# GLA state block on TensorE: a chunk's four attention products ahead of its four state products, one opening product per PSUM bank

## The chip, the cores and the metric

The kernel runs on one NeuronCore of a Trainium2 chip. The metric is the device time of one execution in microseconds (us); lower is better. Times of several runs are given as a median.

## What is computed

The reference is one layer of a decoder trunk with four parallel token mixers over 1024 tokens and 1024 features. The mixer that matters here is gated linear attention (GLA), 4 heads, key width 64, value width 128, run chunk by chunk. Cut to what matters (`qt`, `kt`, `vt` are a chunk's queries, keys and values, `cum` the running sum of the log gates, `decay` its causal differences):

```
o_inter = einsum('bhtk,bhkv->bhtv', qt * exp(cum), state)
att     = einsum('bhtk,bhsk,bhtsk->bhts', qt, kt, decay)
o       = o_inter + einsum('bhts,bhsv->bhtv', att, vt)
state   = exp(last) * state + einsum('bhsk,bhsv->bhkv', kt * exp(last - cum), vt)
```

So each chunk's output of each head is a sum of two matrix products: attention weights times values, contracted over the chunk's tokens, and the decayed queries times the state, contracted over the 64 key features. Then each head is normalised, gated and stored.

## The kernel before

The program runs in blocks, one after another, with a barrier of all engines between two blocks: the front (projections, convolution), stick-breaking attention, GLA, windowed attention, the merge and the MLP. Through the middle blocks TensorE also works off the gate projection, `Dense` (names `dn_...`), in pieces: `dense.pieces(pe, 1)` issues 6 or 9 instructions of `split_product` (lines 661 to 663, 128x512 each), while `dense.serve` on ScalarE copies finished halves out and splits the next weights (lines 156 and 135), `dense.lower` on GpSimd makes their low part (line 139) and `dense.move` on the SP queue stores and loads. Where a piece stands between other work is written out by hand in each block.

`stage_gla` has four blocks: preparation, the attention levels (line 1836, into `gl_ps_att`), the **state block** (lines 1886 to 1955) and the norm block (lines 1957 on). A chunk is 128 tokens (`CH`), so there are `N_CH` = 8. Head h has the numbers c = h // 2 and r = h % 2. A head's 64 key features lie in partitions 0 to 63 for r = 0 and 64 to 127 for r = 1.

In the state block the order on TensorE is, for n = 0 to 7:

1. `update(n)` (n < 7, line 1909): four products of keys and values into `gl_ps_u`. Each uses 64 columns of the array: head r writes partitions 64r to 64r + 63. The first weight load waits for `state_ready`.
2. for n < 6 one piece of the gate projection;
3. waits for `o_copied` (the output bank of chunk n - 2 copied out by ScalarE) and for `state_ready` (both halves of the state before chunk n);
4. for each of four heads an **attention product** (line 1926, `gl_ps_o<-gl_att,gl_v_tok`, all 128 rows of the array) and, for n >= 1, a **state product** (line 1929, `gl_ps_o<-gl_q_decayed,gl_state`, 64 rows of the array) that accumulates on it. Heads with r = 0 write one PSUM bank, heads with r = 1 another; the two heads of a bank (c = 0, 1) write its columns 0 to 127 and 128 to 255. The last product increments `o_done`.

VectorE makes the next state from `update(n)` once the outputs of chunk n - 1 are done (lines 1942, 1945; two instructions a chunk). ScalarE copies each chunk's output to `gl_oT` (line 1953). An fp32 product shows in the profile as two instructions (passes), so a chunk's 8 products are 16 rows. In the profile `64*128` in front of a shape means 64 rows and 128 columns of the array, `128*64` means 128 rows and 64 columns.

The norm block then runs, per head, Square and three other instructions on ScalarE (lines 1981 to 1984), a sum on TensorE over the squares (line 1999) after two pieces of the gate projection, and Ln and Exp of that sum on ScalarE (lines 1986, 1987).

Of the kernel before, what the change touches and what calls it, by code (L numbers as in the profile page):

```python
# [13 lines left out]
P = 128  # L14
# [35 lines left out]
def sems(nc, ctx, *names):  # L50

    Kernel.in_use += [nc.alloc_semaphore(n) for n in names]
    return Kernel.in_use[-len(names):]
# [9 lines left out]
def feature_tiles(ap):  # L63

    return ap.rearrange("(t p) c -> p t c", p=P)
# [1179 lines left out]
E = 64  # L1245
# [378 lines left out]
GLA_HEADS = 4  # L1624
GLA_TAU = 16.0
CH = P
# [4 lines left out]
def stage_gla(nc, k, w_gate, dense):  # L1631
# [7 lines left out]
    with ExitStack() as outer:  # L1639
        def hold(name, shape, dt=F32):  # L1640
            return outer.enter_context(nc.sbuf_tensor(name, shape, dt))
# [4 lines left out]
        q_in = hold("gl_q_decayed", [P, 2, S])  # L1646
        k_tok = hold("gl_k_tok", [P, N_CH, 2 * P])
        v_tok = hold("gl_v_tok", [P, N_CH, GLA_HEADS * P])
        last_decay = hold("gl_last", [P, 2, N_CH])
        with ExitStack() as ctx:  # L1650
# [14 lines left out]
            @block.sync  # L1665
            def _(sp):
                sp.wait_ge(k.stick_stored, 32)
                dense.finish(sp, dense.first_gate - R_CONV)
                sp.dma_start(low[:, :], k.proj[R_LOW * P:R_LOW * P + RANK, :]).then_inc(low_in, 16)
                sp.dma_start(wg[:, :], w_gate[0]).then_inc(low_in, 16)  # L1670
                sp.dma_start(vT[:, :, :], feature_tiles(k.proj[R_CV * P:(R_CV + 4) * P, :])).then_inc(v_in, 16)
                sp.dma_start(q[:, :, :], feature_tiles(k.proj[R_CQ * P:(R_CQ + 2) * P, :])).then_inc(qk_in, 16)
                sp.dma_start(kk[:, :, :], feature_tiles(k.proj[R_CK * P:(R_CK + 2) * P, :])).then_inc(qk_in, 16)
                dense.move(sp, FROM + PREPARE)
# [91 lines left out]
        att = hold("gl_att", [P, N_CH // 2, 2, HALF])  # L1766
# [115 lines left out]
        with ExitStack() as late:  # L1882
# [3 lines left out]
            with ExitStack() as ctx:  # L1886
                state = ctx.enter_context(nc.sbuf_tensor("gl_state", [P, 2, 2, P], F32))
                ps_o = ctx.enter_context(nc.psum_tensor("gl_ps_o", [P, 2, 2, HALF], F32))
                ps_u = ctx.enter_context(nc.psum_tensor("gl_ps_u", [P, 2, HALF], F32))
                update_done, state_ready, o_done, o_copied = sems(nc, ctx, "gl_update_done", "gl_state_ready", "gl_o_done", "gl_o_copied")  # L1890
                block = ctx.enter_context(nc.Block())

                @block.sync
                def _(sp):
                    sp.dma_start(rT[:, :, :], feature_tiles(k.proj[R_CR * P:(R_CR + 4) * P, :])).then_inc(r_in, 16)
                    dense.move(sp, FROM + PREPARE + LEVEL + STATE)

                @block.gpsimd
                def _(pool):
                    dense.lower(pool, FROM + PREPARE + LEVEL + STATE)  # L1900

                @block.tensor
                def _(pe):
                    def update(n):
                        if n >= 2:
                            pe.wait_ge(state_ready, 2 * (n - 1))
                        for h in range(GLA_HEADS):
                            c, r = h // 2, h % 2
                            last = nc.tensor.matmul(ps_u[E * r:E * r + E, n % 2, c * P:(c + 1) * P],
                                                    k_tok[:, n, c * P + E * r:c * P + E * r + E], v_tok[:, n, h * P:(h + 1) * P],  # L1910
                                                    start=True, stop=True)
                        last.then_inc(update_done, 1)

                    for n in range(N_CH):
                        if n < N_CH - 1:
                            update(n)
                        if n < 3 * STATE:
                            dense.pieces(pe, 1)
                        if n >= 2:
                            pe.wait_ge(o_copied, n - 1)  # L1920
                        if n >= 1:
                            pe.wait_ge(state_ready, 2 * n)
                        for h in range(GLA_HEADS):
                            c, r = h // 2, h % 2
                            dst = ps_o[:, n % 2, r, c * P:(c + 1) * P]
                            last = nc.tensor.matmul(dst, v_tok[:, n, h * P:(h + 1) * P],
                                                    att[:, n // 2, r, (2 * (n % 2) + c) * P:(2 * (n % 2) + c + 1) * P], start=True, stop=(n == 0))
                            if n >= 1:
                                last = nc.tensor.matmul(dst, state[E * r:E * r + E, n % 2, c, :], q_in[E * r:E * r + E, c, n * CH:(n + 1) * CH],
                                                        start=False, stop=True)  # L1930
                        last.then_inc(o_done, 1)

                @block.vector
                def _(dve):
                    for n in range(N_CH - 1):
                        dve.wait_ge(update_done, n + 1)
                        if n >= 1:
                            dve.wait_ge(o_done, n)
                        for c in range(2):
                            new = state[:, (n + 1) % 2, c, :]  # L1940
                            if n == 0:
                                ins = nc.vector.tensor_copy(new, ps_u[:, n % 2, c * P:(c + 1) * P])
                            else:
                                dve.wait_ge(state_ready, 2 * n)
                                ins = nc.vector.scalar_tensor_tensor(out=new, in0=state[:, n % 2, c, :], scalar=last_decay[:, c, n:n + 1],
                                                                     in1=ps_u[:, n % 2, c * P:(c + 1) * P], op0=ALU.mult, op1=ALU.add)
                            ins.then_inc(state_ready, 1)

                @block.scalar
                def _(act):  # L1950
                    for n in range(N_CH):
                        act.wait_ge(o_done, n + 1)
                        nc.scalar.activation(oT[:, :, n * CH:(n + 1) * CH].rearrange("p (c r) t -> p r c t", r=2),
                                             ps_o[:, n % 2, :, 0:2 * P].rearrange("p r (c t) -> p r c t", t=P), ACT.Copy).then_inc(o_copied, 1)
                        dense.serve(act, FROM + PREPARE + LEVEL + min((n + 1) // 3, STATE))
# [379 lines left out]
```

## Time and profile before

| | |
|---|---|
| device time, median of 3 runs | 2219.93 us (2217.63 to 2221.23) |
| device time of the profiled execution | 2223.6 us |
| its span, first to last instruction | 2221.9 us |
| mean granted TensorE clock | 0.978 |
| TensorE (PE) busy | 2108.0 us, 95% of the span |
| VectorE (DVE) busy | 943.6 us, 42% |
| ScalarE (ACT) busy | 651.3 us, 29% |
| GpSimd (POOL) busy | 542.2 us, 24% |
| state block on TensorE | from 915.50 to about 955.1 us |

PEld is the loading of weights, which overlaps the products. The granted clock is a share of full speed: 1.00 is 2.4 GHz and 0.50 is 1.2 GHz. A busy time over a stretch shows occupancy only: two instructions that run beside each other, or one that waits in the pipe for another, count as busy all the same. Distances between the starts of two rows tell more, and the tables below are read in that way.

### The profile page before, as it was taken

The page shows a single profiled execution, that of the slowest core. Times are in us where ns is not written, and L with a number is a line of the kernel's source. Part 1 is how long each engine was busy: PE and PEld are TensorE (multiplying, and loading weights), DVE is VectorE, ACT ScalarE, POOL GpSimd, SP SyncE. Part 2 cuts the span into 40 slices and gives each one's busy share as a digit, 9 for nine tenths or more (in the row PEclk, how much of TensorE's full clock was granted, in tenths as well). Part 3 has the DMA queues.
Part 4 walks back from the last instruction along what each step waited for, and adds up shares of the span by engine and source line. Part 5 has one row for each costly group of instructions (what it writes and reads, how often), then busy time and mean ns, then how long its engine had stood idle before and what let it go on. Part 6 is the DMA issues. An engine that isn't in the chain of part 4 may idle for free. (4 is left out here: it accounts for less than half of the span.)

```text
span 2221.9 us, 23815 instructions
## 1 busy us (share of the span) xinstructions
PE 2108.0 (95%) x9584; PEld 1664.3 (75%) x9584; DVE 943.6 (42%) x1109; ACT 651.3 (29%) x913; POOL 542.2 (24%) x260
## 2 busy tenths in 40 slices
PE   6999999999999989988998799699999999999999
PEld 5878888787655668765787678478888888888887
DVE  6455753012333366333543368453343333334324
ACT  5311111233445222154653233232221221122111
POOL 0112222211211133014201011301343343333332
PEclk9999999999999989999999899899999999999999
DMA  8345553333111411235114476600111111111112
GB/s 276 100 139 167 151 152 95 91 106 122 38 42 39 153 57 39 77 106 193 37 59 142 145 239 218 255 20 20 48 48 48 48 48 57 48 39 52 53 48 95
DMA packets 200550, 216.99 MB, mean 98 GB/s; under 512 B 8778, under 2 KB 156362, under 8 KB 200442
## 3 DMA queue, kind: packets, MB, share of 16 engines
q1 hardware_dynamic: 200272, 215.40, 30.3%
q8 instruction: 77, 1.26, 0.2%
q14 instruction: 31, 0.25, 0.0%
q10 hardware_dynamic: 170, 0.07, 0.0%
HBM read 162.85 MB, written 52.59 MB: 97 GB/s over the span
## 5 line engine op out<-in xcount | busy, mean ns | idle before, releaser
L661 PE MATMUL dn_ps<-h_hi,dn_hi 128*128 128x512 f32 (+1 forms) x1120 | 470.5, 420 | 18.8 <-PEq L60 8.2
L663 PE MATMUL dn_ps<-h_hi,dn_lo 128*128 128x512 f32 (+1 forms) x1120 | 443.3, 396 | 0.0
L662 PE MATMUL dn_ps<-h_lo,dn_hi 128*128 128x512 f32 (+1 forms) x1120 | 442.9, 395 | 0.0
L139 POOL TENSOR_TENSOR dn_lo<-dn_raw,dn_hi 128x1024 fp32r<-128x1024 f32 (+1 forms) x69 | 166.0, 2406 | 691.2 <-ACT dn_hi L135 571.9
L661 PEld LDWEIGHTS dn_ps<-h_hi,dn_hi 128*128 128x128 f32 (+1 forms) x1120 | 213.0, 190 | 92.5 <-issue 41.6
L662 PEld LDWEIGHTS dn_ps<-h_lo,dn_hi 128*128 128x128 f32 (+1 forms) x1120 | 213.3, 190 | 49.5 <-issue 7.2
L663 PEld LDWEIGHTS dn_ps<-h_hi,dn_lo 128*128 128x128 f32 (+1 forms) x1120 | 212.5, 190 | 49.2
L1200 DVE TENSOR_TENSOR tl_x<-tl_x,tl_bank 128x512 f32<-128x512 f32 x256 | 173.2, 686 | 133.1 <-PE tl_bank L663 133.1
L156 ACT ACTIVATE dn_out<-dn_ps 128x512 f32<-128x512 f32 (+1 forms) x138 | 81.9, 593 | 476.3 <-PE dn_ps L663 469.9
L1036 POOL TENSOR_TENSOR tl_w_lo<-tl_raw,tl_w_hi 128x1024 fp32r<-128x1024 f32 x64 | 153.4, 2397 | 231.1 <-ACT tl_w_hi L957 231.1
L661 PE MATMUL tl_bank<-tl_h_hi,tl_w_hi 128*128 128x512 f32 x512 | 199.5, 390 | 0.0
L662 PE MATMUL tl_bank<-tl_h_lo,tl_w_hi 128*128 128x512 f32 x512 | 199.2, 389 | 0.0
L663 PE MATMUL tl_bank<-tl_h_hi,tl_w_lo 128*128 128x512 f32 x512 | 199.2, 389 | 0.0
L661 PE MATMUL tl_bank<-tl_w_hi,tl_u_hi 128*128 128x512 f32 x512 | 199.2, 389 | 0.0
L662 PE MATMUL tl_bank<-tl_w_lo,tl_u_hi 128*128 128x512 f32 x512 | 199.2, 389 | 0.0
L663 PE MATMUL tl_bank<-tl_w_hi,tl_u_lo 128*128 128x512 f32 x512 | 199.2, 389 | 0.0
L1042 POOL TENSOR_TENSOR tl_u_lo<-tl_square,tl_u_hi 128x1024 fp32r<-128x1024 f32 x32 | 104.3, 3259 | 277.5 <-DVE tl_square L1190 277.5
L1190 DVE TENSOR_TENSOR tl_square<-tl_relu 128x1024 f32<-128x1024 f32 x32 | 39.6, 1239 | 306.5 <-ACT tl_relu L988 306.5
L957 ACT ACTIVATE tl_w_hi<-tl_raw 128x1024 fp32r<-128x1024 f32 x64 | 67.8, 1061 | 286.2 <-PE tl_bank L663 226.6
L663 PEld LDWEIGHTS tl_bank<-tl_h_hi,tl_w_lo 128*128 128x128 f32 x512 | 96.1, 188 | 20.0
L661 PEld LDWEIGHTS tl_bank<-tl_h_hi,tl_w_hi 128*128 128x128 f32 x512 | 96.1, 188 | 20.0
L661 PEld LDWEIGHTS tl_bank<-tl_w_hi,tl_u_hi 128*128 128x128 f32 x512 | 96.1, 188 | 19.9
(281 smaller groups left out, 2969.3 us busy)
## 6 DMA issues: line engine op xcount, KB each, us to landing
dn_raw<-w_in_dram SPq DMA_DIRECT2D x70, 512.0 KB, 4.3
ada<-w_ada_dram SPq DMA_DIRECT2D x24, 1024.0 KB, 7.3
proj<-dn_out SPq DMA_DIRECT2D x72, 256.0 KB, 2.2
logits<-dn_out SPq DMA_DIRECT2D x64, 256.0 KB, 2.1
mg_gate<-logits SPq DMA_DIRECT2D x32, 512.0 KB, 5.1
tl_raw<-w_up_dram SPq DMA_DIRECT2D x32, 512.0 KB, 3.9
tl_raw<-w_down_dram SPq DMA_DIRECT2D x32, 512.0 KB, 3.5
wa_qk<-proj SPq DMA_DIRECT2D x6, 1024.0 KB, 16.5
```

Source lines behind the costliest of these rows:

```text
L139: self.nc.gpsimd.tensor_tensor(self.lo_at(j), self.raw_at(j), self.hi_at(j).bitcast(F32), ALU.subtract).then_inc(self.lo_ready, 1)
L156: self.nc.scalar.activation(self.out[0:width, h, :], self.ps[0:width, h, :], ACT.Copy).then_inc(self.copied, 1)
L661: nc.tensor.matmul(out, w_hi[:, t, :], x_hi[:, t, :], start=begin, stop=False)
L662: nc.tensor.matmul(out, w_hi[:, t, :], x_lo[:, t, :], start=False, stop=False)
L663: mm = nc.tensor.matmul(out, w_lo[:, t, :], x_hi[:, t, :], start=False, stop=end)
L957: nc.scalar.activation(dst, raw[:, ring(j)], ACT.Copy).then_inc(hi_ready, 1)
L1036: nc.gpsimd.tensor_tensor(lo, raw[:, ring(j)], hi.bitcast(F32), ALU.subtract).then_inc(lo_ready, 1)
L1042: nc.gpsimd.tensor_tensor(u_lo[:, b % 2, f, :], square[:, n % 2], u_hi[:, b % 2, f, :].bitcast(F32), ALU.subtract).then_inc(u_lo_ready, 1)
L1190: nc.vector.tensor_tensor(square[:, n % 2], relu[:, n % 2], relu[:, n % 2], ALU.mult).then_inc(square_ready, 1)
L1200: nc.vector.tensor_tensor(x1[:, tt, cols], x1[:, tt, cols], bank[:, 4 + n % 4, :], ALU.add).then_inc(summed, 1)
```

## The change

In step 4 the four attention products of a chunk now come first, then the wait for `state_ready`, then the four state products. The state products' order is h = 0, 1, 2, 3 as before, so r alternates 0, 1, 0, 1. Since the first product of a bank clears what is accumulated in the whole bank, only c = 0 opens (`start=(c == 0)`), and c = 1 writes its own columns without opening. The number of instructions and their operands stay; all other engines' code stays.

```
@@ -1918,16 +1918,17 @@
                             dense.pieces(pe, 1)
                         if n >= 2:
                             pe.wait_ge(o_copied, n - 1)
+                        for h in range(GLA_HEADS):
+                            c, r = h // 2, h % 2
+                            last = nc.tensor.matmul(ps_o[:, n % 2, r, c * P:(c + 1) * P], v_tok[:, n, h * P:(h + 1) * P],
+                                                    att[:, n // 2, r, (2 * (n % 2) + c) * P:(2 * (n % 2) + c + 1) * P],
+                                                    start=(c == 0), stop=(n == 0), skip_group_check=True)
                         if n >= 1:
                             pe.wait_ge(state_ready, 2 * n)
-                        for h in range(GLA_HEADS):
-                            c, r = h // 2, h % 2
-                            dst = ps_o[:, n % 2, r, c * P:(c + 1) * P]
-                            last = nc.tensor.matmul(dst, v_tok[:, n, h * P:(h + 1) * P],
-                                                    att[:, n // 2, r, (2 * (n % 2) + c) * P:(2 * (n % 2) + c + 1) * P], start=True, stop=(n == 0))
-                            if n >= 1:
-                                last = nc.tensor.matmul(dst, state[E * r:E * r + E, n % 2, c, :], q_in[E * r:E * r + E, c, n * CH:(n + 1) * CH],
-                                                        start=False, stop=True)
+                            for h in range(GLA_HEADS):
+                                c, r = h // 2, h % 2
+                                last = nc.tensor.matmul(ps_o[:, n % 2, r, c * P:(c + 1) * P], state[E * r:E * r + E, n % 2, c, :],
+                                                        q_in[E * r:E * r + E, c, n * CH:(n + 1) * CH], start=False, stop=True, skip_group_check=True)
                         last.then_inc(o_done, 1)
```

TensorE's order before, from the end of the state block's chunk 5 to the block's end (`x4` is four products of one kind in a row):

```order
L1909 MATMUL gl_ps_u<-gl_v_tok,gl_k_tok 64x128 x4
L1926 MATMUL gl_ps_o<-gl_att,gl_v_tok 128x128
L1929 MATMUL gl_ps_o<-gl_q_decayed,gl_state 128x128
L1926 MATMUL gl_ps_o<-gl_att,gl_v_tok 128x128
L1929 MATMUL gl_ps_o<-gl_q_decayed,gl_state 128x128
L1926 MATMUL gl_ps_o<-gl_att,gl_v_tok 128x128
L1929 MATMUL gl_ps_o<-gl_q_decayed,gl_state 128x128
L1926 MATMUL gl_ps_o<-gl_att,gl_v_tok 128x128
L1929 MATMUL gl_ps_o<-gl_q_decayed,gl_state 128x128
L1926 MATMUL gl_ps_o<-gl_att,gl_v_tok 128x128
L1929 MATMUL gl_ps_o<-gl_q_decayed,gl_state 128x128
L1926 MATMUL gl_ps_o<-gl_att,gl_v_tok 128x128
```

In each chunk from 1 to 7 the two kinds alternate product by product.

TensorE's order of the change at the same place, chunks 5, 6 and 7 and the barrier (line 1923 is the attention product, line 1930 the state product):

```order
L1923 MATMUL gl_ps_o<-gl_att,gl_v_tok 128x128 x4
L1930 MATMUL gl_ps_o<-gl_q_decayed,gl_state 128x128 x4
L1909 MATMUL gl_ps_u<-gl_v_tok,gl_k_tok 64x128 x4
L1923 MATMUL gl_ps_o<-gl_att,gl_v_tok 128x128 x4
L1930 MATMUL gl_ps_o<-gl_q_decayed,gl_state 128x128 x4
L1923 MATMUL gl_ps_o<-gl_att,gl_v_tok 128x128 x4
L1930 MATMUL gl_ps_o<-gl_q_decayed,gl_state 128x128 x4
L1886 UNCONDITIONAL_BRANCH
```

Eight changes of kind within a chunk have become two. Of the pieces of the gate projection and of `update` none has moved, and the other four engines' orders are the same.

## Rows read from the trace of the kernel before

**Rows 1.** The page: busy time, share and instructions of each engine.

```profile
PE 2108.0 (95%) x9584; PEld 1664.3 (75%) x9584; DVE 943.6 (42%) x1109; ACT 651.3 (29%) x913; POOL 542.2 (24%) x260
```

**Rows 2.** Waits in the state block (915 to 955.2 us): who, on whom, us, times, longest.

```profile
DVE gl_state L1945 <- PE gl_ps_u L1909: 28.8, 6, 5.4
ACT gl_oT L1953 <- PE gl_ps_o L1929: 27.0, 6, 5.4
```

**Rows 3.** Timeline of TensorE, chunk 0: start, us, engine, line, names, shape.

```profile
915.50 0.66 PE L1909 MATMUL gl_ps_u<-gl_v_tok,gl_k_tok 128*64 128x128 f32 x8 [1.65 <-PEq L1767]
...
918.27 1.05 PE L1926 MATMUL gl_ps_o<-gl_att,gl_v_tok 128*128 128x128 f32 x8
919.25 0.66 PE L1909 MATMUL gl_ps_u<-gl_v_tok,gl_k_tok 128*64 128x128 f32 x8
919.84 0.50 PE L661 MATMUL dn_ps<-h_hi,dn_hi 128*128 128x512 f32 x1
```

**Rows 4.** The same, chunk 1, first and last products, and what follows.

```profile
922.02 0.38 PE L1926 MATMUL gl_ps_o<-gl_att,gl_v_tok 128*128 128x128 f32 x2
922.34 0.49 PE L1929 MATMUL gl_ps_o<-gl_q_decayed,gl_state 64*128 64x128 f32 x2
...
925.25 0.66 PE L1909 MATMUL gl_ps_u<-gl_v_tok,gl_k_tok 128*64 128x128 f32 x8
```

**Rows 5.** The same, start of chunk 6, start of chunk 7, end of the block.

```profile
948.43 0.49 PE L1926 MATMUL gl_ps_o<-gl_att,gl_v_tok 128*128 128x128 f32 x2
...
951.76 0.49 PE L1926 MATMUL gl_ps_o<-gl_att,gl_v_tok 128*128 128x128 f32 x2
...
954.68 0.49 PE L1929 MATMUL gl_ps_o<-gl_q_decayed,gl_state 64*128 64x128 f32 x2
956.25 0.76 PE L661 MATMUL dn_ps<-h_hi,dn_hi 128*128 128x512 f32 x1 [1.09 <-PEq L1886]
```

**Rows 6.** Timeline of TensorE, windowed attention: products that alternate row halves.

```profile
1067.05 0.71 PE L1448 MATMUL wa_ps_s<-wa_qk 64*128 64x128 f32 x8 [2.53 <-PEq L1288]
1067.70 0.50 PE L661 MATMUL dn_ps<-h_hi,dn_hi 128*128 128x512 f32 x1
...
1105.79 1.30 PE L1448 MATMUL wa_ps_s<-wa_qk 64*128 64x128 f32 x8
1107.02 0.55 PE L1459 MATMUL wa_ps_t<-ident,wa_prob 128*128 128x128 f32 x3
```

**Rows 7.** Timeline of VectorE, state block: the state before chunk 7.

```profile
948.55 0.60 DVE L1945 SCALAR_TENSOR_TENSOR gl_state<-gl_state,gl_last,gl_ps_u 128x128 f32<-128x128 f32 x2 [4.70 <-PE gl_ps_u L1909]
```

**Rows 8.** Timeline of ScalarE, state block, after chunk 5.

```profile
947.95 0.60 ACT L1953 ACTIVATE gl_oT<-gl_ps_o 128x512 f32<-128x512 f32 x1 [4.71 <-PE gl_ps_o L1929]
948.44 0.59 ACT L156 ACTIVATE dn_out<-dn_ps 128x512 f32<-128x512 f32 x1
948.92 1.06 ACT L135 ACTIVATE dn_hi<-dn_raw 128x1024 fp32r<-128x1024 f32 x1
```

**Rows 9.** Stretches: us, busy PE, PEld, DVE, ACT, POOL (x instructions), granted clock, DMA share, GB/s.

```profile
951.80:955.20 3.40, 3.37 (x17) 2.33 (x16) 0.00 (x0) 0.60 (x1) 0.00 (x0) 1.00 0.00 0
955.20:956.20 1.00, 0.00 (x0) 0.00 (x0) 0.00 (x0) 0.71 (x2) 0.11 (x1) 0.67 0.00 0
956.20:959.00 2.80, 2.75 (x7) 2.20 (x8) 0.00 (x0) 2.77 (x3) 2.27 (x1) 0.50 0.00 0
...
973.80:975.40 1.60, 0.23 (x2) 0.03 (x1) 1.60 (x2) 1.60 (x3) 0.00 (x0) 1.00 1.12 332
...
991.70:994.60 2.90, 0.21 (x1) 0.00 (x0) 0.30 (x1) 1.54 (x2) 0.00 (x0) 1.00 0.61 242
```

**Rows 10.** Timeline of TensorE, norm block, pieces for the first head.

```profile
956.82 0.63 PE L662 MATMUL dn_ps<-h_lo,dn_hi 128*128 128x512 f32 x1
...
962.36 0.41 PE L663 MATMUL dn_ps<-h_hi,dn_lo 128*128 128x512 f32 x1
```

**Rows 11.** Timeline of ScalarE, norm block, Ln of the first head's sum.

```profile
965.22 1.12 ACT L1986 ACTIVATE gl_att<-gn_ps,eps 128x1024 f32<-128x1024 f32 x1 [4.96 <-PE gn_ps L1999]
```

## The prediction

> **What bounds the kernel now.** I began with the busy shares [rows 1]: TensorE is busy for 95% of the span and no other engine for half of it, so time taken off TensorE's stream comes off the whole, unless another wait takes its place. Next I asked who waits in the state block [rows 2]. VectorE and ScalarE wait for TensorE, 28.8 and 27.0 us in total; TensorE waits for neither of them there. The block is therefore as long as its row of products, and the timeline of TensorE is the view that matters. In it one looks at the distances between starts, since all these rows read as busy.
>
> **What the alternation costs.** In chunk 0 there is no state yet, and the four attention products run one behind another: from 918.27 to the start of the next kind at 919.25, 0.98 us [rows 3]. This takes in the change to the other kind of array shape that follows. In chunk 1 the eight alternating products run from 922.02 to 925.25, 3.23 us [rows 4]. A product costs 3.23 / 8 = 0.40 us there, against 0.98 / 4 = 0.245 us in chunk 0, although half of them use only half the rows. So what is paid for is the change of shape between full height and half height, eight times a chunk (the step to `update` is the eighth). The chunks 2 to 5 repeat this; chunk 6 runs from 948.43 to 951.76 and chunk 7 about as long, 3.33 us [rows 5], since they have no gate piece ahead and are entered through one more change of shape.
>
> **The change, part by part.**
>
> *Attention products together.* They become what chunk 0 has: 0.98 us, with the change of shape behind them [rows 3].
>
> *State products together, row halves alternating.* No place in the state block shows this. The nearest rows are in windowed attention, where four products of 64 rows and 128 columns alternate between the halves just as these will (h % 2, each half to banks of its own): 1067.05 to 1067.70, 0.65 us, with the change of shape behind them in it [rows 6]. Bounds: from below, `update`, four products that share the array by columns, 919.25 to 919.84, 0.59 us [rows 3]. From above, four products that share nothing: 0.98 us as in chunk 0, plus 0.10 us for entering from another shape (3.33 less 3.23), 1.08 us. Another row of the same line is dearer still, 1105.79 to 1107.02, 1.23 us [rows 6], but its operands are read with a step between elements, and `state` and `q_in` are read without one. I take 0.65: same shape, same alternation, same kind of access.
>
> *Sum.* A chunk's products fall from 3.23 to 0.98 + 0.65 = 1.63 us, by 1.60 us. In chunks 6 and 7 both sides carry the extra 0.10. Seven chunks: 7 x 1.60 = **11.2 us**. By the bounds it is 7 x (3.23 - 0.98 - 0.59) = 11.6 at best, 7 x (3.23 - 0.98 - 1.08) = 8.2 if the halves take turns, and 7 x (3.23 - 0.98 - 1.23) = 7.1 by the dearest row.
>
> The Trainium skill, page "TensorE: Matmul & The Clock Gate", section "Measured speedup vs the span model", gives a dimmer view of packing: four row tiles measured 3.07 times one, not 4. An estimate by that share (0.77) would make the paired products some 0.1 us dearer a chunk and the saving about 0.7 us smaller; the row at 1067.05 does not show such a loss.
>
> *The waits.* The wait for `o_copied` stays in front, the wait for `state_ready` moves back by 0.98 us, so neither can come to bind later than before by its place alone; but the block is shorter, so I follow both to the tightest chunk. The state before chunk 7 is made at 948.55, 0.12 us behind `update`, and takes 0.60 us [rows 7]. In the new order chunk 6's 1.7 us and chunk 7's attention products lie between, so it is ready some 2 us early. The output bank that chunk 7 wants is copied at 947.95 to 948.55 [rows 8], and chunk 7 starts about 1.7 us behind `update`. ScalarE then has 1.5 us of gate work queued, to 949.98 [rows 8]; chunk 6 would end at 948.43 + 1.73 = 950.2, and its copy is waited for by nobody before the end. Cover is thus there for all of VectorE's and ScalarE's work. If it were gone, the price is the 0.60 us of one copy. The increment of `o_done` is on the last product as before. Fewer changes of shape touch no queue, and nothing is moved past a DMA.
>
> *The clock behind the block.* After the last product, at 954.68, TensorE has nothing until 956.25 [rows 5], where the barrier ends. In that gap the granted clock goes from 1.00 to 0.50 (2.4 to 1.2 GHz) and stays low over the next pieces [rows 9]. Two gaps that are longer, 973.8 to 975.4 and 991.7 to 994.6, leave it at 1.00 [rows 9]. What differs is what the engine did before: there pieces of the gate projection without pause, here 6.7 us of alternation. In the new order the last two chunks are packed half as wide in time, so I expect the clock to stay. Price: between 956.25 and 962.36 there are 14 pieces' instructions in 6.11 us [rows 5, 10]; at full speed nine of them take 2.18 us (919.84 to 922.02, [rows 3, 4]), so 14 take 2.18 + 5 x 0.23 = 3.34. That is **2.8 us**, and it lies on the path, since ScalarE waited 4.96 us for the sum behind these pieces [rows 11].
>
> So 11.2 + 2.8 = 14.0 us. The profiled execution took 2223.6 us, which would become 2209.6. It is 3.7 us above the median of the runs, 2219.93, and 2.4 above the slowest; I carry the saving over to the median: 2219.93 - 14.0 = **2205.9 us**. The blocks that follow start from a barrier and are moved as a whole, so I take nothing off for them.
>
> **The rivals.**
>
> *The clock falls all the same* (or falls elsewhere instead). For it: the gap before the norm block stays 1.6 us long. Then only 11.2 us go: 2208.7 us. Chance 0.27.
>
> *The row halves take turns* while accumulating. For it: the row that I rely on opens its outputs, here each product adds to what stands in the bank. Against it: each half has a bank of its own. Saving 7.1 to 8.2 us, 2211.7 to 2212.8 us. Chance 0.10.
>
> The Trainium skill, page "TensorEngine Tiling (Array Packing)", section "Gotcha 1: PSUM Pressure", says that row tiles may not use one PSUM bank at the same time. Here r chooses both the half and the bank, so it would not apply.
>
> *The gain is lost behind the block,* in a wait for a transfer that ends when it always did, or because the change of shape is no shorter in groups (the change then does not do what it says). Nothing in the waits speaks for it. 2219.9 us. Chance 0.04.
>
> *Slower: the denser products bring TensorE's clock down within the block.* At the low clock a gate instruction takes (962.36 - 956.82) / 13 = 0.43 us [rows 10] instead of 0.23. The block runs from 915.50 [rows 3] to about 955.1 [rows 5]; its new 28.4 us (39.6 less 11.2) would grow by about 0.85 of themselves, 24 us, and the end would be 2219.93 - 11.2 + 24 = 2232.7 us. It decides from the point at which 11.2 / 0.85 = 13 us of the block's work run low. Against it: the clock was 1.00 in the alternation and held through two gaps behind dense pieces [rows 9]. Chance 0.02.
>
> **How the numbers follow.** Forecast 0.57, rivals 0.27, 0.10, 0.04 and 0.02. A measurement of this kernel tells about 0.2% (4.4 us) from no change. The first three cases are all faster by more than that: 0.94; same 0.04; slower 0.02. The range begins below the forecast by the spread of the runs shown (3.6 us): 2202.3. It ends at the dearest price of the paired products, 2212.8.
>
> **What would show it.** In the profile of the changed kernel: four attention products start 0.98 us ahead of the state products; the state products start in pairs, 0.65 us for four; a chunk's eight take 1.6 us; the state block on TensorE runs from about 915.5 to 943.9; ScalarE's wait for the first sum is 2.2 instead of 4.96 us and the clock behind the block stays 1.00. It is wrong if the state products take over 1 us for four, if TensorE shows a wait for `gl_state` or `gl_oT`, or if the later blocks, laid beside the old ones, are longer by several us.

## The result, and the profile after

The change makes the kernel faster: 2207.78 us as the median of 5 runs (2206.23 to 2211.13) against 2220.08 us (2217.63 to 2221.23) before, a ratio of 0.9948 with a 95% interval of 0.9933 to 0.9963. That is 12.3 us less, between 8 and 15 by the interval. The forecast was 2205.9 us in a range of 2202.3 to 2212.8.

The page of the changed kernel, whose profiled execution took 2207.0 us (span 2205.2):

```profile
PE 2093.2 (95%) x9584; PEld 1655.1 (75%) x9584; DVE 943.7 (43%) x1109; ACT 651.1 (30%) x913; POOL 544.1 (25%) x260
```

Against [rows 1], TensorE is busy for 14.8 us less with as many instructions, and no other engine's busy time moved by more than 2 us. Its timeline (start, us, engine, line, names, array and shape), chunk 1, then chunks 6 and 7 and the start of the norm block:

```profile
921.94 1.05 PE L1923 MATMUL gl_ps_o<-gl_att,gl_v_tok 128*128 128x128 f32 x8
922.92 0.71 PE L1930 MATMUL gl_ps_o<-gl_q_decayed,gl_state 64*128 64x128 f32 x8
923.57 0.66 PE L1909 MATMUL gl_ps_u<-gl_v_tok,gl_k_tok 128*64 128x128 f32 x8
...
940.35 1.16 PE L1923 MATMUL gl_ps_o<-gl_att,gl_v_tok 128*128 128x128 f32 x8
941.43 0.72 PE L1930 MATMUL gl_ps_o<-gl_q_decayed,gl_state 64*128 64x128 f32 x8
942.08 1.16 PE L1923 MATMUL gl_ps_o<-gl_att,gl_v_tok 128*128 128x128 f32 x8
943.17 0.71 PE L1930 MATMUL gl_ps_o<-gl_q_decayed,gl_state 64*128 64x128 f32 x8
944.98 0.47 PE L661 MATMUL dn_ps<-h_hi,dn_hi 128*128 128x512 f32 x1 [1.10 <-PEq L1886]
```

Read against [rows 4]: four attention products take 922.92 - 921.94 = 0.98 us, four state products 923.57 - 922.92 = 0.65 us, together 1.63 us where eight alternating ones took 3.23. Chunk 6 takes 942.08 - 940.35 = 1.73 us against 3.33 [rows 5]. The last state group starts at 943.17; the last pair of rows of the block before started at 954.68 [rows 5]. The first start of the next block is at 944.98 instead of 956.25: 11.27 us earlier. The block itself began 0.08 us earlier (915.42 instead of 915.50 [rows 3]), so 11.2 us are the block's.

The waits of the changed kernel in the block (who, on whom, us, times, longest):

```profile
DVE gl_state L1946 <- PE gl_ps_u L1909: 20.8, 6, 3.8
ACT gl_oT L1954 <- PE gl_ps_o L1930: 18.6, 7, 3.8
...
PE gl_ps_u L1909 <- PEq L1767: 1.6, 1, 1.6
PE dn_ps L661 <- PEq L1886: 1.1, 1, 1.1
```

VectorE and ScalarE still wait for TensorE, for less time than in [rows 2]; TensorE waits for the two barriers and for nothing else. ScalarE's timeline over the last chunks is the answer to [rows 8]:

```profile
939.88 0.60 ACT L1954 ACTIVATE gl_oT<-gl_ps_o 128x512 f32<-128x512 f32 x1 [3.11 <-PE gl_ps_o L1930]
940.37 0.59 ACT L156 ACTIVATE dn_out<-dn_ps 128x512 f32<-128x512 f32 x1
940.85 1.06 ACT L135 ACTIVATE dn_hi<-dn_raw 128x1024 fp32r<-128x1024 f32 x1
942.20 0.60 ACT L1954 ACTIVATE gl_oT<-gl_ps_o 128x512 f32<-128x512 f32 x1 [0.29 <-PE gl_ps_o L1930]
...
951.09 1.12 ACT L1987 ACTIVATE gl_att<-gn_ps,eps 128x1024 f32<-128x1024 f32 x1 [2.08 <-PE gn_ps L2000]
```

The copy of chunk 6 had 0.29 us of idle time ahead of it (942.20): ScalarE was done with its gate work by so much before chunk 6 was. The wait for the first sum of the norm block is 2.08 us instead of 4.96 [rows 11]. The clock, in stretches of the changed kernel (us, busy PE, PEld, DVE, ACT, POOL, granted clock, DMA share, GB/s):

```profile
943.20:944.90 1.70, 0.68 (x9) 0.49 (x8) 0.00 (x0) 0.69 (x2) 0.08 (x1) 1.00 0.00 0
944.90:949.20 4.30, 4.22 (x19) 3.52 (x20) 0.00 (x0) 4.04 (x4) 2.32 (x1) 1.00 0.01 4
...
979.70:986.50 6.80, 5.97 (x14) 4.79 (x15) 3.63 (x14) 0.00 (x0) 0.65 (x2) 0.50 0.88 315
```

It stayed at 1.00 behind the block, as forecast, so at the end of the norm block the profiled execution is 14.1 us ahead: 11.3 at its start and 2.8 more by the clock. It then fell to 0.50 at the start of windowed attention, where the kernel before had 1.00 (994.6 to 1005.0 us), and the lead fell to 11.3 us. That did not last either: further on TensorE waits for a transfer in the kernel before, and not in the changed one.

```profile
1021.57 1.17 PE L1357 MATMUL wa_ps_v<-ident,wa_vT 128*128 128x128 f32 x8 [3.08 <-DMA wa_vT<-proj]
...
1007.34 1.16 PE L1357 MATMUL wa_ps_v<-ident,wa_vT 128*128 128x128 f32 x8
```

The first row is of the kernel before, the second the same one of the changed kernel: 1021.57 - 1007.34 = 14.2 us ahead again. So what the low stretch at 979.7 us had cost was time that the wait would have taken. At the first product of the tail (the block that holds the MLP, names `tl_...`) the lead is 15.3 us. Whether the clock behind the state block has anything to do with the change is the question that was left to the runs.

### The profile page after: what moved, and what is told of

Its sections match the earlier page's. It is cut to its first block and busy times, and to the rows that moved or that the text cites. A ratio compares the mean times of both kernels' runs of the same rounds, so it can differ in the third digit from the quotient of the medians.

```text
span 2205.2 us, 23809 instructions
## 1 busy us (share of the span) xinstructions
PE 2093.2 (95%) x9584; PEld 1655.1 (75%) x9584; DVE 943.7 (43%) x1109; ACT 651.1 (30%) x913; POOL 544.1 (25%) x260
```

## The experiments

What was to be told apart: how much of the 11.2 us comes from fewer changes of array shape and how much from halves that run beside each other; whether the alternation of halves is what lets them; whether the opening flag plays a part; and whether the low clock belongs to the old order. All block lengths below are from the first start of line 1909 (`update`) to the start of the block's last TensorE instruction, which the merged rows shown here do not list by itself; it is 39.39 us in the kernel before and 28.19 us in the changed kernel. Where the clock was low for a while inside the block, that is said.

### The flag alone

```
-                            last = nc.tensor.matmul(dst, v_tok[:, n, h * P:(h + 1) * P],
-                                                    att[...], start=True, stop=(n == 0))
+                            nc.tensor.matmul(dst, v_tok[:, n, h * P:(h + 1) * P],
+                                             att[...], start=(c == 0), stop=False, skip_group_check=True)
```

The diff is against the kernel before; the state product stays behind each attention product.

> The kernel before in its order of products (attention, state, attention, state), and only the flag changed: c = 0 alone opens a bank. Theory (the flag itself is free, all of the gain is in the order): 3.23 us for a chunk's eight products, the kernel before's time, 2220 us within 3 us. Rival (opening twice costs something): below 3.1 us a chunk. If what the clock does behind the block hangs on the alternation ahead of the gap, it falls to 0.50 behind the block as in the kernel before and the wait of ScalarE for the first sum of the norm block is near 5 us; if it is chance, it may stay at 1.00 and the wait is near 2 us.

Measured: 2221.94 us (10 runs) against 2222.24 us, ratio 0.9997 (0.9988 to 1.0006). The block was 40.98 us long, with the clock low inside it for a while:

```profile
920.00:923.40 3.40, 3.40 (x12) 2.85 (x12) 0.00 (x0) 0.00 (x0) 0.79 (x1) 0.50 0.98 377
...
960.90:964.40 3.50, 3.50 (x9) 2.75 (x10) 0.00 (x0) 3.44 (x4) 2.08 (x1) 0.51 0.00 0
```

The 1.59 us more than 39.39 are what that low stretch costs: from the block's start to chunk 1's first attention product it is 6.52 us in the kernel before and 8.11 here, and 8.11, 8.12 and 8.13 in the three more runs below that have it at this place. The flag is free. The clock fell behind the block here too; ScalarE waited 3.7 us for its first sum.

### Two and two

```
+                        for c in range(2):
+                            for r in range(2):
+                                h = 2 * c + r
+                                last = nc.tensor.matmul(ps_o[:, n % 2, r, c * P:(c + 1) * P], v_tok[:, n, h * P:(h + 1) * P],
...
+                            if n >= 1:
+                                if c == 0:
+                                    pe.wait_ge(state_ready, 2 * n)
+                                for r in range(2):
+                                    last = nc.tensor.matmul(ps_o[:, n % 2, r, c * P:(c + 1) * P], state[E * r:E * r + E, n % 2, c, :],
...
```

These loops stand in place of the changed kernel's two loops over h.

> The changed kernel with a chunk's products in twos: two attention products (heads 0, 1), two state products (heads 0, 1), then the same for heads 2, 3: four changes of shape a chunk instead of two (eight before). If each change of shape costs the same and the halves still pair up: two attention products 0.54 us (0.64 where entered from the other shape), two state products 0.42 us, a chunk's eight 2.0 us, so 7 x 1.2 = 8.5 us below the kernel before, near 2211.5 us. Rival (two state products are too few to run beside each other): 0.54 to 0.64 us for two, 2.4 us a chunk, 5.5 us below the kernel before, near 2214.5 us.

TensorE's timeline, chunk 1:

```profile
922.04 0.61 PE L1924 MATMUL gl_ps_o<-gl_att,gl_v_tok 128*128 128x128 f32 x4
922.58 0.49 PE L1931 MATMUL gl_ps_o<-gl_q_decayed,gl_state 64*128 64x128 f32 x4
923.00 0.71 PE L1924 MATMUL gl_ps_o<-gl_att,gl_v_tok 128*128 128x128 f32 x4
923.64 0.49 PE L1931 MATMUL gl_ps_o<-gl_q_decayed,gl_state 64*128 64x128 f32 x4
924.06 0.66 PE L1909 MATMUL gl_ps_u<-gl_v_tok,gl_k_tok 128*64 128x128 f32 x8
```

The steps are 0.54, 0.42, 0.64 and 0.42 us, 2.02 in all, each as worked out ahead. The block is 30.94 us: 2.75 more than the change's for 14 more changes of shape, **0.20 us each**. Time: 2213.3 us, ratio 0.9959 (0.9944 to 0.9975), 9 us below the kernel before on that chip.

### No changes of shape within a chunk

```
-                                last = nc.tensor.matmul(dst, state[E * r:E * r + E, n % 2, c, :], q_in[E * r:E * r + E, c, n * CH:(n + 1) * CH],
+                                last = nc.tensor.matmul(dst, state[:, n % 2, c, :], q_in[:, c, n * CH:(n + 1) * CH],
```

The diff is against the kernel of the first experiment (alternating order).

> The kernel before's alternating order (with c = 0 alone opening a bank), but each state product runs over all 128 rows of state and decayed queries instead of its head's 64; it leaves out the separation of the two heads of a pair, so its outputs mix them. Theory (the change of array shape is what the alternation pays): no shape changes are left within a chunk, and eight products cost 8 x 0.224 + 0.09 = 1.9 us instead of 3.23. Rival (it is the switching between other weights, other operands or two products on the same output that costs): near 3.2 us as before.

TensorE's timeline, the first two products of chunk 1 and what follows its eight:

```profile
922.17 0.38 PE L1926 MATMUL gl_ps_o<-gl_att,gl_v_tok 128*128 128x128 f32 x2
922.39 0.39 PE L1928 MATMUL gl_ps_o<-gl_q_decayed,gl_state 128*128 128x128 f32 x2
...
924.04 0.66 PE L1909 MATMUL gl_ps_u<-gl_v_tok,gl_k_tok 128*64 128x128 f32 x8
```

Eight products that alternate between attention and state, between two banks and between operands, take 924.04 - 922.17 = 1.87 us. Twice the rows in the state products, and 1.36 us less than the kernel before, for seven changes of shape fewer: 0.19 us each. So the alternation of products costs nothing; the alternation of shapes is the whole of what it costs. One run of each: 2209.61 us beside 2222.16.

### The halves kept from running beside each other

```
-                                last = nc.tensor.matmul(ps_o[:, n % 2, r, c * P:(c + 1) * P], state[E * r:E * r + E, n % 2, c, :],
-                                                        q_in[E * r:E * r + E, c, n * CH:(n + 1) * CH], start=False, stop=True, skip_group_check=True)
+                                last = nc.tensor.matmul(ps_o[:, n % 2, r, c * P:(c + 1) * P], state[0:E, n % 2, c, :],
+                                                        q_in[0:E, c, n * CH:(n + 1) * CH], start=False, stop=True, skip_group_check=True)
```

> The changed kernel, but all four state products of a chunk take their operands from the lower 64 partitions; it leaves out the upper half's state and queries. The two halves can no longer run beside each other, and the number of shape changes is that of the change. Theory: four state products 1.08 to 1.1 us instead of 0.65, a chunk's eight about 2.07; so pairing is worth 0.44 us a chunk, 3.1 us in all, and the fewer shape changes the other 8.2 us. Rival (pairing is worth nothing, the profile's rows merely overlap): 0.65 us again.

TensorE's timeline, chunk 2:

```profile
926.56 1.05 PE L1923 MATMUL gl_ps_o<-gl_att,gl_v_tok 128*128 128x128 f32 x8
927.54 1.16 PE L1930 MATMUL gl_ps_o<-gl_q_decayed,gl_state 64*128 64x128 f32 x8
928.63 0.66 PE L1909 MATMUL gl_ps_u<-gl_v_tok,gl_k_tok 128*64 128x128 f32 x8
```

1.09 us for four instead of 0.65. The block is 32.85 us, of which some 1.6 are a low clock from 920.0 to 923.4 us, so 31.3 us and 3.1 us above the change's 28.19. The 11.2 us are thus **3.1 us of pairing and 8.1 us of shape changes**, 42 of them (six a chunk in seven chunks), 0.19 us each, which agrees with the 0.20 and the 0.19 above. The rows give the pairing by themselves too, without a correction for the clock: 7 x (1.09 - 0.65) = 3.1 us. One run of each: 2214.03 us beside 2222.16.

### Does TensorE need the alternation of halves?

```
-                            for h in range(GLA_HEADS):
+                            for h in (0, 2, 1, 3):
                                 c, r = h // 2, h % 2
                                 last = nc.tensor.matmul(ps_o[:, n % 2, r, c * P:(c + 1) * P], state[E * r:E * r + E, n % 2, c, :],
```

> The changed kernel with the four state products of a chunk in the order h = 0, 2, 1, 3, so that the two of the lower row half come first and the two of the upper half after them; everything else as in the change. Theory A (the gain has two parts: fewer changes of shape, and halves that run beside each other because they alternate): the four state products take about 0.98 + 0.10 = 1.08 us instead of 0.65, a chunk's eight products 2.0 to 2.1 us instead of 1.63, and of the 11.2 us of the block some 3 us come back: about 8.2 us below the kernel before, near 2211 us. Rival B (TensorE finds the other half by itself, whatever the order): 0.65 to 0.75 us for four, and the time of the change, near 2208 us.

TensorE's timeline, chunk 1:

```profile
922.10 1.05 PE L1923 MATMUL gl_ps_o<-gl_att,gl_v_tok 128*128 128x128 f32 x8
923.08 0.72 PE L1930 MATMUL gl_ps_o<-gl_q_decayed,gl_state 64*128 64x128 f32 x8
923.73 0.66 PE L1909 MATMUL gl_ps_u<-gl_v_tok,gl_k_tok 128*64 128x128 f32 x8
```

0.65 us again, and a block of 28.24 us; 2208.63 us, ratio 0.9936 (0.9913 to 0.9958). Theory A fell: with two products of a half in a row TensorE still ran the other half's beside them. That the halves overlap is needed, that they alternate one by one is not.

### The same thing where four of a half stand in a row

The block of attention levels (line 1836) issues four products of the lower half and then four of the upper.

```
-                        for r in range(2):
-                            rows = slice(E * r, E * r + E)
-                            for a in range(2):
-                                for c in range(2):
...
-                            last.then_inc(scored, 1)
+                        for a in range(2):
+                            for c in range(2):
+                                tok = slice((2 * m + a) * CH, (2 * m + a + 1) * CH)
+                                for r in range(2):
+                                    rows = slice(E * r, E * r + E)
...
+                                    if (a, c) == (1, 1):
+                                        last.then_inc(scored, 1)
```

> The changed kernel, and in the block before it (attention levels, line 1836) the 64-row products alternate between the row halves too, instead of four of the lower half and then four of the upper. Theory (alternation is what pairs them up): a group of 8 products takes about 1.1 us instead of 1.64 and the double group about 2.0 instead of 2.74, some 1.9 us a level; in the last six of eight levels TensorE does not wait for VectorE, so 8 to 13 us go on top of the change: near 2197 us. Rival (VectorE's masked copies take over as the bound of the levels, or TensorE already overlaps the halves as far as it can): under 3 us on top, near 2206 us, with new waits of TensorE for gl_att.

One group in the changed kernel, and what follows:

```profile
904.92 1.71 PE L1836 MATMUL gl_ps_att<-gl_parts 64*128 64x128 f32 x16
906.56 0.50 PE L661 MATMUL dn_ps<-h_hi,dn_hi 128*128 128x512 f32 x1
```

A group, and the following row, with the halves alternating:

```profile
896.25 1.16 PE L1836 MATMUL gl_ps_att<-gl_parts 64*128 64x128 f32 x16
897.34 0.50 PE L661 MATMUL dn_ps<-h_hi,dn_hi 128*128 128x512 f32 x1
```

1.64 us become 1.09. From the first product of the levels to the state block it is 98.36 us instead of 111.84 in the changed kernel. TensorE's first wait for the masked copies, early in the block, grew with it, from 8.5 to 11.7 us, and still 13.5 us are left. Time: **2196.18 us**, ratio to the kernel before 0.9882 (0.9867 to 0.9897). Here the order of the halves does count: with four in a row the overlap was only partial. The starts of the single instructions in the changed kernel's group show how far it went: the lower half's first four start alone, at 904.92, 905.13, 905.25 and 905.36 us; its fifth starts at 905.469 and the upper half's first beside it, at 905.475; the upper half's last four are alone again. In the run before, four instructions of one half in a row did not hold the other half back at all (923.080 and 923.093). Both would fit if the other half can start once no more than four instructions of the first are still to start; only these two lengths were tried, so that is a reading and not shown. The edit also moves the lower half's signal to VectorE to the end of the group; what that alone does was not tried.

### Fewer changes of shape still

```
-                        if n < N_CH - 1:
-                            update(n)
+                        if n % 2 == 0:
+                            update(n)
+                            if n + 1 < N_CH - 1:
+                                update(n + 1)
```

> The kernel of e6_levels, and update(n) and update(n + 1) issued one behind the other at each even n, so that a chunk with odd n goes from its state products straight to the gate piece: three changes of shape fewer in the block, some 0.2 us each. Theory: 0.6 us off the block (28.2 to 27.6 us from first to last start), which the times can't tell from e6_levels: near 2196 us. Rival (update(n + 1) now comes before the state it waits for): a wait of TensorE for gl_state ahead of line 1909 and a block as long as or longer than 28.2 us.

> e6_levels again, beside e10_levels_updates and the changed kernel on one chip: 11 to 14 us below the changed kernel, and no low clock right behind the state block if that hangs on what the block does.

TensorE's timeline, chunk 0's products and the gate piece behind them, then chunk 1 and the two updates behind it:

```profile
906.93 1.05 PE L1926 MATMUL gl_ps_o<-gl_att,gl_v_tok 128*128 128x128 f32 x8
907.74 0.48 PE L661 MATMUL dn_ps<-h_hi,dn_hi 128*128 128x512 f32 x1
...
909.88 1.05 PE L1926 MATMUL gl_ps_o<-gl_att,gl_v_tok 128*128 128x128 f32 x8
910.86 0.72 PE L1933 MATMUL gl_ps_o<-gl_q_decayed,gl_state 64*128 64x128 f32 x8
911.50 1.09 PE L1910 MATMUL gl_ps_u<-gl_v_tok,gl_k_tok 128*64 128x128 f32 x16
912.53 0.50 PE L661 MATMUL dn_ps<-h_hi,dn_hi 128*128 128x512 f32 x1
```

The block is 27.57 us instead of 28.19, 0.62 us less. The expectation counted three changes of shape fewer, but there are four: behind chunk 2 and chunk 4 a change to half width and one back become one, while behind chunk 0 both go, since its products and the gate piece have the same shape (the first two rows). So it is 0.62 / 4 = 0.16 us each: the forecast time came out with a wrong count, and changes at the half-width updates are cheaper than the 0.19 to 0.20 between full and half height. TensorE shows no wait for the state. Times: 2193.87 us (0.9876; 0.9862 to 0.9889) beside 2194.94 us (0.9880; 0.9866 to 0.9893) for the kernel without this edit on the same chip; the two can't be told apart by time, and both beat the change and the kernel before. The changed kernel took 2209.53 us on this chip (below), so the order of the levels is worth 14.6 us by the times, slightly more than the 11 to 14 expected, and 13.5 by the block.

### The clock behind the block

> The changed kernel with chunks 6 and 7 in the alternating order and chunks 1 to 5 grouped. The block is 5/7 of the way: 5 x 1.6 = 8.0 us shorter than before's 39.4, 31.4 us from first to last start. If the clock behind the block falls because the last 6.7 us ahead of the gap are alternation, it falls here as in the kernel before, and the wait of ScalarE for the first sum is between 3.5 and 5 us. If what counts is chance, it may stay at 1.00 with a wait of 2.1 us.

> The mirror: chunks 1 to 5 alternate, chunks 6 and 7 are grouped. The block is 2 x 1.6 = 3.2 us shorter than before's, 36.2 us from first to last start. If the alternation just ahead of the gap makes the clock fall, it stays at 1.00 behind the block and the wait of ScalarE for the first sum is 2.1 us; if all of the block's alternation counts, or chance, it may fall.

> The kernel before again, for its clock: if the low clock behind the state block belongs to this kernel, it is there a third time (it was in the first profile and in e5_flags_only's) with a wait of ScalarE for the first sum of 3.5 to 5 us; if it is chance, the wait may be 2.1 us.

> The changed kernel again, with nothing altered: 11 to 14 us below the kernel before. In the block 28.2 us from first to last start, or 29.8 where the clock falls inside it. Whether a low clock follows the block, the norm block or none is open.

The first two are mixtures of the orders, with the chunks that alternate given by `n >= 6` and by `1 <= n < 6`. Their blocks were 32.99 and 37.79 us, each with 1.6 us of low clock inside; without it 31.4 and 36.2, as the sum of 1.6 us a grouped chunk has it. Stretches of the run in which chunks 6 and 7 alternate:

```profile
920.20:923.70 3.50, 3.50 (x13) 2.96 (x12) 0.00 (x0) 0.00 (x0) 0.92 (x1) 0.52 0.97 338
...
944.00:951.70 7.70, 7.70 (x49) 5.55 (x48) 0.60 (x2) 2.63 (x4) 0.00 (x0) 1.00 0.09 34
951.70:953.10 1.40, 0.32 (x2) 0.15 (x3) 0.00 (x0) 0.76 (x2) 0.16 (x1) 1.00 0.00 0
953.10:957.30 4.20, 4.19 (x19) 3.47 (x19) 0.00 (x0) 3.97 (x4) 2.25 (x1) 1.00 0.02 4
```

The last two chunks alternate for over 6 us ahead of the gap, and the clock holds at 1.00 in it and behind it. And the kernel before, taken again without any edit:

```profile
958.30:959.60 1.30, 0.24 (x2) 0.05 (x1) 0.00 (x0) 0.74 (x2) 0.13 (x1) 1.00 0.00 0
959.60:964.00 4.40, 4.34 (x19) 3.62 (x20) 0.00 (x0) 3.99 (x4) 2.27 (x1) 1.00 0.02 4
```

Its block is 39.39 us again, and the clock does not fall behind it; ScalarE waits 2.13 us for the first sum, as after the change. The changed kernel, taken again, has a block of 28.19 us, a wait of 2.08 us and a time of 2209.53 us against 2222.10 us, ratio 0.9947 (0.9933 to 0.9960). So the old order alone does not settle it: of three profiled executions in which all chunks alternate, the low stretch followed the block in two. It followed it in neither of the two mixtures, and in none of the nine in which no chunk alternates shapes product by product. That the old order makes it more frequent is compatible with these counts; that it does is **not settled**, nor is what it would be worth in the end, since the low stretches behind the block differ from execution to execution of one kernel (in the two profiles of the changed kernel the first one after the block begins at 979.7 and at 1006.9 us).

## Why the prediction was right

**The sum of the block: right to 0.1 us (11.2 forecast, 39.39 - 28.19 = 11.20 measured).** 0.98 and 0.65 us a chunk were forecast and measured, as was the extra 0.10 in chunks 6 and 7. The choice of 0.65 between 0.59 and 1.23 rested on one row of another block with the same shape, the same halves and operands without a step [rows 6], and that row carried over exactly, though it opened its outputs and these accumulate. The bound for halves that take turns, 1.08, was also right: the run that forces it measured 1.09.

**The reason: right in its main part, too narrow in one.** Changes of shape are what was paid for (full-height products in the old order cost 1.87 us), at 0.19 to 0.20 us each, 8.1 of the 11.2 us; the other 3.1 are the halves beside each other. The prediction leaned on the halves alternating one by one "just as these will"; two products of a half in a row do as well, four in a row, in the block of the levels, do not.

**The waits: right.** Nothing took the place of the removed time in the block. ScalarE's gate work was forecast to end 0.2 us before chunk 6 (949.98 against 950.2), and it ended 0.29 us before.

**The rivals.** Halves that take turns: excluded. A gain lost behind the block: none of size; from the first start behind the block to the first product of the tail it is 442.7 us in the profile before and 438.7 in the one after, but 440.2 and 440.9 in the two taken again, so that stretch varies by itself and says nothing about the change. Slower by a low clock in the block: the block did lose 1.6 us in four profiles of other kernels, one of them in the old order, by a low stretch of 3.4 us, far from the 13 us of work it would have taken.

**The clock behind the block: the step that failed.** "What differs is what the engine did before" took one execution's low stretch for a trait of the kernel. The price was sized rightly for that execution: between the first two profiles the lead does grow by 2.8 us in the norm block, and it is still there at the tail. But the low stretch was absent in the kernel before when it was taken again, and between that pair nothing is gained there: ScalarE waits 2.13 and 2.08 us. Alternation just ahead of the gap was also not enough for a fall (the run with chunks 6 and 7 alternating). What is shown as the change's own is 11.2 us; a share of the low stretches may belong to it too, by the counts above, and stays open. The first rival, the clock falling all the same or elsewhere, with 2208.7 us, was thus nearer to what was measured (2207.78) than the forecast, 2205.9. The measured 12.3 and 12.6 us can't decide between them: their intervals hold 11.2 as well as 14.0. That the forecast came so near in spite of a term of 2.8 us that the repeat did not show is in part luck.

## What to carry to other kernels

When TensorE is the bound, look at the distances between starts, not at the busy times, wherever products of different height or width follow each other: here each change between full and half height cost 0.2 us, almost as much as a whole 128-column fp32 product (0.22 us). Group products by shape, let the first product of a bank alone open it, and keep products of the two row halves close together, each half with a bank of its own; where four of one half stood in a row, interleaving them was worth more than the change itself. And before a low clock in one profile is counted as a cost of the code, take the same kernel's profile once more, and look whether a wait further on gives the time back.

## What the runs showed of the hardware that was not expected

- TensorE overlapped the two row halves with two products (four instructions) of one half in a row, 0.65 us for four as with strict alternation; with four in a row a group of eight took 1.64 us instead of 1.09, and the upper half's first instruction started beside the fifth of the lower half, ahead of three that stand before it in the program.
- A change between full and half height came to the same in three runs that get at it by different ways: 0.19, 0.19 and 0.20 us. The four changes at the half-width updates that another run left out came to 0.16 us on average.
- The granted clock fell to 0.50 for some 3.4 us at 920 us in four of the fourteen profiled executions, just behind the start of the state block, in kernels that do not differ before that point. Each time it cost the block 1.6 us. All four had come to the block some 3 us late, at 918.3 to 918.8 us where six others of the kernels that are the same up to there came at 915.4 to 915.6; the repeat of the kernel before came at 918.9 and did not have it.
- A low stretch need not cost what its products lose: the one at 979.7 us in the changed kernel took 2.8 us off its lead, and 3.08 us of waiting for a transfer in the kernel before gave them back.
